# Decay sums of the linear attention: one fp32 product replaced by two rounded products

## The reference, cut to what matters

```
la = log_sigmoid(r @ w_decay + b_decay) / 16        # log decays, (tokens, 128)
bcum = cumsum(la)
o_inter = (q * exp(bcum)) @ s
att[t,s] = sum_d q[t,d] k[s,d] exp(bcum[t,d] - bcum[s,d])   for s <= t
o = o_inter + att @ v
s_new = exp(b_last) * s + (k * exp(b_last - bcum))^T @ v
```

## Time and profile before

| | us |
|---|---|
| median of 3 runs | 4437.72 |
| the runs | 4439.46, 4423.33, 4437.72 |
| the profiled execution | 4428.45 |
| its span | 4426.6 |
| PE busy in it | 4076.0 (92%) |
| PEld, POOL, DVE, ACT busy | 3124.9, 1791.9, 1601.8, 1045.7 |

### The profile page before, as it was taken

The page is one execution under the profiler, slowest core; times in us unless marked ns, Lnnn a source line. Parts: engine busy times, 40 slices in busy tenths (PEclk is TensorE's granted clock), DMA queues, the critical chain, the costliest instruction groups (busy, mean ns, idle before and its releaser), DMA issues. The chain is left out here.

```text
span 4426.6 us, 52348 instructions
## 1 busy us (share of the span) xinstructions
PE 4076.0 (92%) x19915; PEld 3124.9 (71%) x19915; DVE 1601.8 (36%) x2487; ACT 1045.7 (24%) x1771; POOL 1791.9 (40%) x770
## 2 busy tenths in 40 slices
PE   6999999999989999799899998888798998999999
PEld 5777788888878887566677776766585545877744
DVE  1343325555632132333324555344313554122100
ACT  2433212222210001433222222000225663011000
POOL 1333342332335445243454333766442211887600
PEclk7899999999999999899999999999887997999999
DMA  6111221111135533222222111323422110333322
GB/s 181 42 41 49 74 50 44 47 40 48 40 91 115 103 88 96 62 50 53 67 64 58 48 47 51 89 72 99 140 49 53 36 32 19 95 100 81 90 78 74
DMA packets 512282, 305.19 MB, mean 69 GB/s; under 512 B 37769, under 2 KB 492818, under 8 KB 511210
## 3 DMA queue, kind: packets, MB, share of 16 engines
q1 hardware_dynamic: 500010, 282.43, 26.1%
q10 hardware_dynamic: 12096, 20.33, 1.3%
HBM read 276.42 MB, written 26.27 MB: 68 GB/s over the span
## 5 line engine op out<-in xcount | busy, mean ns | idle before, releaser
L850 POOL TENSOR_TENSOR whi<-ring,con 128x1024 fp32r<-128x1024 f32 (+2 forms) x383 | 891.4, 2327 | 2358.7 <-DMA ring<-in_w_in 1863.8
L539 PE MATMUL ps<-xT_parts,whi 128*128 128x512 f32 (+2 forms) x2600 | 1011.1, 389 | 101.7 <-DVE arena L2033 39.9
L539 PE MATMUL ps<-hT_parts,whi 128*128 128x512 f32 (+1 forms) x2856 | 1055.4, 370 | 0.0
L539 PE MATMUL ps<-xT_parts,ring_parts 128*128 128x512 f32 (+2 forms) x2600 | 954.3, 367 | 0.0
L852 POOL TENSOR_TENSOR ring_parts<-ring,whi 128x1024 fp32r<-128x1024 f32 (+2 forms) x383 | 902.3, 2356 | 30.0
L1535 ACT ACTIVATE arena<-ps 128x512 f32<-128x512 f32 (+7 forms) x583 | 311.8, 544 | 2253.3 <-PE ps L539 1509.0
L539 PE MATMUL ps<-arena_parts,whi 128*128 128x512 f32 (+1 forms) x2112 | 640.0, 380 | 70.4 <-DVE arena_parts L2065 60.6
L539 PE MATMUL ps<-arena 128*128 128x128 f32 (+9 forms) x3292 | 649.5, 342 | 28.9 <-DVE arena L2033 23.3
L539 PEld LDWEIGHTS ps<-xT_parts,whi 128*128 128x128 f32 (+1 forms) x2600 | 501.2, 193 | 212.0 <-issue 68.6
L539 PEld LDWEIGHTS ps<-hT_parts,whi 128*128 128x128 f32 x2856 | 549.9, 193 | 92.2 <-issue 6.5
L539 PEld LDWEIGHTS ps<-arena 128*128 128x128 f32 (+3 forms) x3292 | 440.4, 194 | 187.2 <-issue 126.7
(11 more groups left out here) (141 smaller groups left out, 3572.8 us busy)
## 6 DMA issues: line engine op xcount, KB each, us to landing
ring<-in_w_in SPq DMA_DIRECT2D x504, 256.0 KB, 3.9
arena<-in_w_ada SPq DMA_DIRECT2D x64, 256.0 KB, 4.8
ring<-in_w_up SPq DMA_DIRECT2D x64, 256.0 KB, 4.0
ring<-in_w_down SPq DMA_DIRECT2D x64, 256.0 KB, 3.6
ring<-in_w_out SPq DMA_DIRECT2D x48, 256.0 KB, 3.7
gates_kept<-stage ACTq DMA_DIRECT2D x24, 384.0 KB, 3.9
arena<-gates_kept SPq DMA_DIRECT2D x24, 384.0 KB, 3.9
ring<-in_w_ada SPq DMA_DIRECT2D x32, 256.0 KB, 4.0
```

The source lines that it names most:

```text
L539: return nc.tensor.matmul(o, l, r, start=first, stop=last)
L850: v.tensor_tensor(hi, raw, ones[:, 0:m].unsqueeze(1).to_broadcast([P, kt, m]), ALU.mult).then_inc(w_rounded, 1)
```

## The change

Of the log decays, DVE now writes the result of its combination into `gtmp`, copies it into `gla` as a rounded part (fp32r) and puts the rest of it, also rounded, into `gtmp`. The constant matrix `sums` is rounded once, in place, ahead of the first head of layer 0. `exponents` makes, for each stretch of columns, one fp32r product with the high part and one with the low part, added up in PSUM. Its wait for `la_ready` is per direction now and stands inside `exponents`. `gam` gets storage of its own. The three stores of bias rows in the second block write 639 columns of a row in place of 640.

```diff
-        con = sb("con", [P, C_COLS])
+        con = sb_twins("con", [P, C_COLS])
...
-        gam = gtmp.rearrange("p a b -> p (a b)")[:, 0:8 * P].rearrange("p (l t) -> p l t", l=8)
+        gam = take(8, P)
+        gla_parts = as_part(gla), as_part(gtmp.rearrange("p d (t m) -> p d t m", t=NT))
+        sums_part = as_part(sums)
...
-                    pe.wait_ge(la_ready, hh * 2 + 2)
-
                     def exponents(j):
...
                         pe.wait_ge(kN_ready, u0 + j)
-                        if full:
-                            for c, w in ((0, 512), (1, 512), (2, P)):
-                                last = mm(bank(2 + c, w), gla[:, d, t], sums[:, d, c * 512:c * 512 + w], True, True)
-                        else:
-                            for c, k in ((0, 0), (2, 8)):
-                                last = mm(bank(2 + c, P), gla[:, d, t], sums[:, d, k * P:(k + 1) * P], True, True)
+                        pe.wait_ge(la_ready, hh * 2 + d + 1)
+                        pieces = [(2 + c, c * 512, w) for c, w in ((0, 512), (1, 512), (2, P))] if full else \
+                            [(2, 0, P), (4, 8 * P, P)]
+                        for c, at, w in pieces:
+                            for h in range(2):
+                                last = mm(bank(c, w), gla_parts[h][:, d, t], sums_part[:, d, at:at + w], h == 0, h == 1)
                         last.then_inc(sum_done, 1)
...
-            nc.scalar.dma_start(rows_dram[0:4], brow[0:4, 0]).then_inc(rows_kept, 16)
-            nc.scalar.dma_start(rows_dram[4:12], brow[4:12, 1]).then_inc(rows_kept, 16)
-            nc.scalar.dma_start(rows_dram[12:20], brow[12:20, 0]).then_inc(rows_kept, 16)
+            nc.scalar.dma_start(rows_dram[0:4, 0:TOE], brow[0:4, 0, 0:TOE]).then_inc(rows_kept, 16)
+            nc.scalar.dma_start(rows_dram[4:12, 0:TOE], brow[4:12, 1, 0:TOE]).then_inc(rows_kept, 16)
+            nc.scalar.dma_start(rows_dram[12:20, 0:TOE], brow[12:20, 0, 0:TOE]).then_inc(rows_kept, 16)
...
+                if l == 0:
+                    own(v.tensor_copy(sums_part, sums))
+                    own.settle()
...
                         dve.wait_ge(dec_ln, hh * 2 + d + 1)
-                        stt(gla[:, d].rearrange("p t m -> p (t m)"), bank(4 + 2 * d, ALL), 0.0, gtmp[:, d], ALU.min,
-                            ALU.subtract).then_inc(la_ready, 1)
+                        own(stt(gtmp[:, d], bank(4 + 2 * d, ALL), 0.0, gtmp[:, d], ALU.min, ALU.subtract))
+                        own.settle()
+                        own(v.tensor_copy(gla_parts[0][:, d].rearrange("p t m -> p (t m)"), gtmp[:, d]))
+                        own.settle()
+                        v.tensor_tensor(gla_parts[1][:, d].rearrange("p t m -> p (t m)"), gtmp[:, d],
+                                        gla_parts[0][:, d].rearrange("p t m -> p (t m)").bitcast(F32),
+                                        ALU.subtract).then_inc(la_ready, 1)
```

## The result

The changed kernel took 4392.14 us in the median of 4 runs (4379.96 to 4392.92), the kernel before 4435.41 us in the median of 4. The ratio is 0.9898, with a 95% interval from 0.9872 to 0.9925: 45 us faster, from 33 to 57. In a second comparison, on another occasion, it was 0.9908 (0.9889 to 0.9927), 41 us. 44 had been forecast.

A forecast was written before the change was run, and what follows sets the result against it. TensorE was taken to bound layer 0, VectorE's loop most of layer 1's units. Savings of 36.4 and 8.4 us, 44.8 less 0.5 for rounding `sums`, gave 44 us and 4390 us; range 4368 to 4416.

The forecast's parts named there:

- The product: Sums of a full unit on TensorE: 1.14 us rounded against 1.93 in fp32, saving 0.80; other units save nothing.
- The layers: Savings summed over the heads of each layer: 36.4 us in layer 0 and 8.4 us in layer 1.
- The floor: Full units cannot go below 7.71 to 7.76 us, so most layer 1 units gain only what they have above that.
- The loop over VectorE: Per unit: levels, then mask, add, and products with q and k; VectorE's part 5.55 us, levels and hand-overs 2.2.
- What was added: VectorE's split of log decays, hidden ahead of the first sums; rounding of `sums` 0.5 us; bias rows' stores nothing.
- No gain in the matmul: Rival, TensorE's sums: a rounded product between fp32 ones takes 0.43 us; 0 us gained or half a microsecond slower; chance 0.05.
- the late hand-over: Rival, layer 0: filled tile free 0.8 us late in each second unit, 19 us lost, 25 us gained; chance 0.07.
- The missing floor: Rival, both layers: VectorE's loop does not hold, all 80 full units save 0.80 us, 64 us gained; chance 0.05.
- The clock: Rival, layer 1's units: TensorE's idle time lowers its clock, 6.3 us more a unit, up to 155 us slower; chance 0.05.

The follow-up runs named there:

- two half-changes: Split and rounded products in layer 0 alone, or layer 1 alone, other layer as in the kernel before: 4395.39 us (ratio 0.9925) and 4422.96 us (0.9982).
- the run with the addition moved: Changed kernel with VectorE's mask addition of a unit placed behind the next unit's q and k products: 4366.65 us, ratio 0.9856 against the kernel before.

## Why the prediction was right

**The product.** The forecast took 0.80 us a full unit; the distances in layer 0 went from 9.36 to 8.55, 0.81. The prices came from rows of matmuls with other operands, and the constant matrix as moving operand changed nothing. That rounded products of 128 columns save nothing can be read in the units of layer 1 that are not full, whose sums are four matmuls of 128 columns and nothing else. TensorE's timeline of the kernel before,

```profile
2415.23 0.68 PE L539 MATMUL ps<-con,arena 128*128 128x128 f32 x4 [0.46 <-ACT arena L1535]
...
2415.99 0.40 PE L539 MATMUL ps<-hT_parts,whi 128*128 128x512 f32 x1
```

and of the changed one:

```profile
2378.62 0.63 PE L541 MATMUL ps<-con_parts,arena_parts 128*128 128x128 f32 x4 [0.41 <-issue]
...
2379.38 0.40 PE L541 MATMUL ps<-hT_parts,whi 128*128 128x512 f32 x1
```

From the first sum to the second matmul of the fill it is 0.76 us in both. Only the Exp came 0.05 us sooner behind its sums (0.67 for 0.72). So the gain is in the long ones, 4 x (0.428 - 0.231) = 0.79 us a unit.

**The layers.** 36.4 and 8.4 us were forecast; the two half-changes gave 33 (22 to 44) and 8 (0 to 15). The traces say it more closely. In head 0 of layer 0 the Exp of unit 0 to that of unit 11 went from 737.30 - 637.00 = 100.30 us to 723.12 - 631.09 = 92.03. That is 8.3; with the sums of unit 0 ahead of it, 0.8, this is the forecast 9.1, and the four heads together give 36.4. In layer 1 the first full unit's Exp to the eighth's went from 56.60, 55.21, 55.20 and 54.74 us to 53.76, 53.63, 53.60 and 53.61. That is 7.2, and with 0.83 a head ahead of it 10.5 us, not 8.4.

**The floor.** The loop over VectorE was rightly found, and that the sums lie beside it; the run without the low part showed that it holds, and the run with the addition moved showed what it is made of. But 7.71 was not this loop. The forecast read it as the lower end of the floor and counted six distances at 7.95 in a head behind one at 7.76. Heads 1 and 2 had 7.71, 7.76 and then five at 7.95, and heads 0 and 3 began with a 7.71 too. That distance had the sums on its path, and not the addition: it went to 6.88 or 6.89 with the short sums, and stayed at 7.71 when only the addition was moved. So 0.83 us a head, 3.3 in all, was missing from the sum for layer 1. Against it, the loop itself takes 7.76 to 7.81 in the other distances and not 7.71 to 7.76, about 1 us over some 25 units. In layer 0 the floor came out at 7.81 between the Exps. By the distances the whole change gives 47 us, by the forecast 44.8, by the two comparisons 45 and 41. That the measured 8 us of layer 1 meets the forecast 8.4 is in part luck, for its interval is 15 us wide.

**What was added.** The split was forecast at 0.67 to 0.96 us an operation, or 3.2 beside POOL; it was 0.56 and 0.96 in each of the 16 splits, with 10 us to spare in head 0. So the copies were below the forecast's bounds, and the slow form did not occur. In head 0 POOL's passes had ended by then. The rounding of `sums` took 1.36 us, below its bounds of 2.0 to 9.6; a POOL pass beside it took 2.63 where others take 2.40, and TensorE shows no wait from it. The 0.5 us that the sum took for it is thus not seen. The bias rows' stores were not tested alone; they are in the run without the rounded products, which showed no change.

**The rivals.** No gain in the matmul and the late hand-over are both refuted by 8.55 in layer 0. The missing floor fell with the runs above: layer 1 alone did not give 26 us. The clock stayed at 1.00 in layer 1's units, though TensorE waits 0.4 us in most, and up to 2.02 us once. That this rival was far off isn't shown: in the run without the low part waits of 1.88 and 2.56 us were followed by a lower clock.

**The profiled execution** was 35.5 us shorter than that of before (4428.45 to 4392.92), not 44. The first levels came 5 us earlier than the change explains (641.00 to 635.1, of which 0.8 is the change's), and so about 14 us were lost elsewhere. One such place can be seen. The end of head 2 of layer 0 has the same work in both. In the 50 us from 1062 us on in the kernel before, TensorE was busy for 45.22 us at a granted clock of 1.00; in the changed one, from 1028 us on, for 45.27 at 0.97. The longest wait of TensorE in it was 2.63 us before and 2.62 after, the same. From the Exp of unit 11 to that of the next head's unit 0 it was 56.95 and 57.71, though the sums in it are 0.8 us shorter. The first head's end went the other way (58.32 to 56.13). Where the rest of the 14 us went was not traced stage by stage. The clock of the whole execution points the same way: it was 0.947 before and 0.942 after. Taking 45 us at full clock off the first would leave 0.946. Of the 23 runs of the kernel before that were made beside the last experiments, the eight at 0.947 or more took 4421 us in the mean, the four at 0.943 and 0.944 took 4441. By this estimate 0.004 less goes with some 19 us, enough for the 14. It is a relation between runs; no experiment set the clock.

## What to carry to other kernels

A shorter product pays in full only where the unit's distance from start to start is TensorE's own; read that distance stage by stage, and look for the engine whose last instruction ends the wait where TensorE has little to do. When a faster step leaves a loop of another engine as the bound, look at that loop's order at once: here an edit that was worth nothing with the slow product gave 20 us with the fast one. Count the columns: the rounded matmul gained only on the wide pieces. And check that a distance taken for a floor really lacks the work that is to be made shorter: the 7.71 us had it.

## What the runs showed of the hardware

A rounding cast of storage to storage on VectorE was faster per element than the operations around it: 128x2304 in 1.36 us, 0.59 ns a column, and 128x768 in 0.56, while a subtraction of the same 128x768 took 0.96.

The same idle time of TensorE (2.62 and 2.63 us) was followed by a clock of 1.00 in one execution and by a lower one in another: 1.00 from 1066 to 1070 us in the kernel before; 0.69 from 1032.4 to 1034.6, 0.57 from there to 1037.0 and 1.00 behind it in the changed one. The first run of ten matmuls behind it shows it at once, as in the changed kernel's timeline of TensorE,

```profile
1032.41 2.20 PE L541 MATMUL ps<-arena 128*128 128x128 f32 x10 [2.62 <-DVE arena L2033]
```

against that of the kernel before:

```profile
1066.40 1.59 PE L539 MATMUL ps<-arena 128*128 128x128 f32 x10 [2.63 <-DVE arena L2033]
```

Ten matmuls took 2.20 us at the lower clock for a part of them, and 1.59 at the higher. Runs of one kernel with a lower mean clock were the longer ones, so this probably makes part of their scatter. Within the run without the low part it was the same: one wait of 1.88 us was followed by 0.65 and one of 1.87 by 1.00.
